# Each 1024-column dot of the expert layer as two instructions of 512 columns

## The reference

```python
experts = e1 * PEER_KEYS + e2                  # 16 of 16384 for each of 8 heads: 128 rows per token
g = jax.nn.softmax(vs, axis=-1)
act = jax.nn.gelu(jnp.einsum('nd,nhkd->nhk', xb, peer_u[experts]), approximate=False)
return jnp.einsum('nhk,nhkd->nd', g * act, peer_v[experts])
```

## Time and profile before

| what | value |
|---|---|
| median of 3 runs | 3529.66 us (3528.91 to 3529.8) |
| profiled execution: its own time | 3546.85 us |
| profiled execution: its span | 3545.1 us |
| busy: PE, DVE, POOL, ACT | 2524.3, 2375.2, 2386.3, 433.4 us |
| DMA | 1321.73 MB, mean 373 GB/s |
| of it gathers | 1107.43 MB |
| mean granted clock of the tensor engine | 0.797 of full speed |

### The profile page before, as it was taken

One profiled execution on the slowest core, in us unless ns is written; L12 is line 12 of the kernel. 1 busy time (PEld: TensorE's weight loads), 2 busy tenths in 40 slices (PEclk: granted clock), 3 DMA queues, 4 the chain that ended last, 5 costly groups with the idle time before them and its releaser, 6 DMA issues.

```text
span 3545.1 us, 35490 instructions
## 1 busy us (share of the span) xinstructions
PE 2524.3 (71%) x11828; PEld 1278.0 (36%) x11828; DVE 2375.2 (67%) x6243; ACT 433.4 (12%) x980; POOL 2386.3 (67%) x2118
## 2 busy tenths in 40 slices
PE   6758566788756786696766677697766777667566
PEld 5634123553432344362332234463332234324100
DVE  4586667767668786867578765767478666847641
ACT  1101100113101221111001110111001110000000
POOL 0155775567757777657767776657767776678876
PEclk8778778898877789897777888898887788766657
DMA  6478999999999999999999999999999999999999
GB/s 251 167 274 317 375 341 408 373 365 377 385 406 341 369 348 410 397 385 388 396 411 408 392 382 407 406 374 400 394 411 396 399 380 407 401 410 403 328 378 353
DMA packets 373369, 1321.73 MB, mean 373 GB/s; under 512 B 60962, under 2 KB 72418, under 8 KB 352962
## 3 DMA queue, kind: packets, MB, share of 16 engines
q0 software_dynamic: 304128, 1107.43, 80.9%
q1 hardware_dynamic: 69058, 212.03, 15.4%
HBM read 1311.41 MB, written 7.88 MB: 372 GB/s over the span
## 4 chain that ended last, share of the span: by engine, by line
POOL 28%; PE 23%; DMA 21%; DVE 14%; issue 11%; SPq 1%; ACT 1%; DVEq 0%; POOLq 0%; ACTq 0%
POOL v_ring L823 14%; POOL u_ring L810 13%; DMA v_ring<-down_rows,codesT 12%; DMA u_ring<-up_rows,codes 6%; PE ps L868 6%; PE ps L931 5%; DMA wbuf<-weights 4%; DVE u_ring L1780 3%; DVE arena L1750 3%; PE ps L921 2%; PE ps L1131 2%; PE ps L1184 2%; DVE idx L1750 1%; DVE top_c L1750 1%; DVE top_v L1750 1%
## 5 line engine op out<-in xcount | busy, mean ns | idle before, releaser
L1780 DVE CUSTOM_DVE_ANT_0 u_ring<-u_ring,xn 128x1024 f32<-128x1024 f32 x1056 | 1263.7, 1220 | 671.1 <-DMA u_ring<-up_rows,codes 670.4
L810 POOL DMA_INDIRECT u_ring<-up_rows,codes x1056 | 1197.0, 1134 | 663.0 <-issue 304.3
L868 PE MATMUL ps<-v_ring,Z 128*32 128x512 f32 x4096 | 1097.8, 755 | 671.9 <-DMA v_ring<-down_rows,codesT 535.0
L823 POOL DMA_INDIRECT v_ring<-down_rows,codesT x1056 | 1188.1, 1125 | 480.2 <-issue 271.7
L868 PEld LDWEIGHTS ps<-v_ring,Z 128*32 128x32 f32 x4096 | 147.3, 120 | 1294.0 <-DMA v_ring<-down_rows,codesT 997.9
L1131 PEld LDWEIGHTS ps<-xT,wbuf 128*128 128x128 f32 x2176 | 309.1, 227 | 185.7 <-issue 118.0
L1131 PE MATMUL ps<-xT,wbuf 128*128 128x128 f32 (+1 forms) x2176 | 334.3, 316 | 47.8 <-DMA wbuf<-weights 47.8
L931 PE MATMUL ps<-wbuf,xT 128*128 128x256 f32 (+2 forms) x1184 | 294.6, 408 | 69.4 <-DMA wbuf<-weights 41.2
L931 PEld LDWEIGHTS ps<-wbuf,xT 128*128 128x128 f32 (+1 forms) x1184 | 231.0, 202 | 150.4 <-DMA wbuf<-weights 45.9
L1750 DVE MAX8 vals<-arena 128x8 f32<-128x128 f32 (+1 forms) x288 | 69.0, 281 | 82.9 <-ACT arena L1564 82.3
L1087 PE MATMUL ps<-kT,qT 96*128 96x512 f32 (+3 forms) x192 | 104.8, 666 | 24.4 <-DVE nb L1754 20.9
(11 more groups left out here) (336 smaller groups left out, 2444.7 us busy)
## 6 DMA issues: line engine op xcount, KB each, us to landing
wbuf<-weights SPq DMA_DIRECT2D x142, 1024.0 KB, 8.2
u_ring<-up_rows,codes POOLq DMA_INDIRECT x1056, 9.0
v_ring<-down_rows,codesT POOLq DMA_INDIRECT x1056, 8.9
u_ring<-weights SPq DMA_DIRECT2D x8, 1024.0 KB, 13.8
v_ring<-weights SPq DMA_DIRECT2D x8, 1024.0 KB, 14.2
wbuf<-weights SPq DMA_DIRECT2D x9, 768.0 KB, 8.2
resid<-x_prompt SPq DMA_DIRECT2D x8, 512.0 KB, 6.8
table<-decay_in SPq DMA_DIRECT2D x8, 512.0 KB, 10.1
```

The costliest lines, as they stand in the source:

```text
L810: pool.indirect_dma_start(out=u_ring[:, i % U_RING, :], out_offset=None, in_=up_rows, in_offset=bass.IndirectOffsetOnAxis(ap=codes[:, t % ...
L823: pool.indirect_dma_start(out=v_ring[:, v % V_RING, :], out_offset=None, in_=down_rows, in_offset=bass.IndirectOffsetOnAxis(ap=codesT[:, t ...
L868: mm = pe.matmul(acc[q:q + 32, half, :], (Zs if t == TILES else Z)[:, at:at + GS], v_ring[:, v % V_RING, half * 512:(half + 1) * 512], sta ...
L1780: dve.tensor_tensor_reduce(u, u, xn[:, t % 2], 1.0, 0.0, ALU.mult, ALU.add, dots[:, k:k + 1]).then_inc(dot_done, 1)
```

## The change

The dot of one slot is done as two instructions, over columns 0 to 511 and 512 to 1023. The first half's sum goes to a new tile `dots_2` (32 columns, one group), the second half's to `dots`, and only the second raises `dot_done`. After the last slot of a group the vector engine waits for that slot's own `dot_done`, adds `dots_2` to `dots` for the 32 columns and raises a new semaphore `dots_summed`, for which the gelu now waits. Ahead of the first slot of a group it waits for its last noted step, so that `dots_2` isn't overwritten while it is still read. A group is GS = 32 slots here (the change's short description speaks of sixteen). The tile `coefs` is gone: the product with the gates is written over `gelus`, and transposed from there.

```diff
--- before.py
+++ after.py
@@ -290,8 +290,8 @@
         codes = sb("codes", [P, 2, SLOTS], U32)
         gates = sb("gates", [P, 2, SLOTS])
         dots = sb("dots", [P, SLOTS])
+        dots_2 = sb("dots_2", [P, GS])
         gelus = sb("gelus", [P, SLOTS])
-        coefs = sb("coefs", [P, SLOTS])
 
         dec_in = table[:, :].rearrange("p (h i) -> p h i", h=H)
         def piece_of(t, w):
@@ -465,6 +465,7 @@
         u_in = [sem(f"u_in_{i}") for i in range(U_RING)]
         v_in = [sem(f"v_in_{i}") for i in range(V_RING)]
         dot_done = sem("dot_done")
+        dots_summed = sem("dots_summed")
         gelu_done = sem("gelu_done")
         coefT_done = sem("coefT_done")
         Z_ready = sem("Z_ready")
@@ -1344,7 +1345,7 @@
 
             def gelu(t, g):
 
-                act.wait_ge(dot_done, t * SLOTS + (g + 1) * GS)
+                act.wait_ge(dots_summed, group_no(t, g) + 1)
                 at = slice(g * GS, (g + 1) * GS)
                 act.activation(gelus[:, at], dots[:, at], ACT.Gelu).then_inc(gelu_done, 1)
 
@@ -1769,16 +1770,24 @@
                 dve.wait_ge(gelu_done, group_no(t, g) + 1)
                 if group_no(t, g) >= 2:
                     dve.wait_ge(Z_ready, group_no(t, g) - 1)
-                do(dve.tensor_tensor, coefs[:, at], gelus[:, at], gates[:, t % 2, at], ALU.mult)
-                do_signal(coefT_done, group_no(t, g) + 1, dve.transpose, coefT[:, g % 2], coefs[:, at])
+                do(dve.tensor_tensor, gelus[:, at], gelus[:, at], gates[:, t % 2, at], ALU.mult)
+                do_signal(coefT_done, group_no(t, g) + 1, dve.transpose, coefT[:, g % 2], gelus[:, at])
 
             def dot(t, k):
 
                 i = t * SLOTS + k
                 dve.wait_ge(u_in[i % U_RING], 16 * (i // U_RING + 1))
-                u = u_ring[:, i % U_RING, :]
-                dve.tensor_tensor_reduce(u, u, xn[:, t % 2], 1.0, 0.0, ALU.mult, ALU.add,
-                                         dots[:, k:k + 1]).then_inc(dot_done, 1)
+                if k % GS == 0:
+                    own.wait()
+                for half, into in ((0, dots_2[:, k % GS:k % GS + 1]), (1, dots[:, k:k + 1])):
+                    of = slice(half * 512, half * 512 + 512)
+                    u = u_ring[:, i % U_RING, of]
+                    ins = dve.tensor_tensor_reduce(u, u, xn[:, t % 2, of], 1.0, 0.0, ALU.mult, ALU.add, into)
+                ins.then_inc(dot_done, 1)
+                if k % GS == GS - 1:
+                    at = slice(k + 1 - GS, k + 1)
+                    dve.wait_ge(dot_done, i + 1)
+                    do_signal(dots_summed, i // GS + 1, dve.tensor_tensor, dots[:, at], dots[:, at], dots_2[:], ALU.add)
 
             def expert_slots(done, upto):
 
```

## The result

The changed kernel takes 3480.01 us in the median of 4 runs (3475.02 to 3489.79), the kernel before 3529.73 in 4 runs beside them: a ratio of 0.9859, with a 95% interval of 0.9835 to 0.9883, so 49.7 us less. The forecast was 42 us less. The profiled execution took 3479.65 us with a span of 3477.9. It lies at the median, where that of the kernel before lay 17 us above its own; spans compared with each other therefore show 67 us, and 17 of these say nothing of the change.

A forecast was written before the change was run, and what follows sets the result against it. The prediction took DMA at 411 GB/s as the main bound, with GpSimd's gather pace in eight stretches. Dots and sums +15 and gathers -57 gave -42 us: 3505 profiled, 3488 without a profile, range 3445 to 3550.

The forecast's parts named there:

- The bound: DMA at 411 GB/s sets most of the time; in eight stretches GpSimd's pace issuing gathers is the bound or very near.
- the eight stretches: Parts of the timeline, 1700 us in all, where GpSimd's busy time plus 0.30 us per gather fills the stretch.
- excess: Gathers' time over 0.938 us each: 404 us in the whole kernel, 252 us of it in the eight stretches.
- The dots' cost: Two instructions add 0.079 us per dot, 83 us; with the sums 94 us, of which +15 on the path.
- The sums: Adding dots_2 to dots for each group of 32: about 0.35 us, 33 times, 11 us; 3 us on the path.
- What the gathers gain: Shorter waits of gathers inside dots: 30% of 404 us, about 120; 76 in the eight stretches, three quarters kept, -57 us.
- The mechanism: A gather begun in a dot waits for its end; caught in the first half, it is freed 0.61 us sooner.
- The lock over the seam: Rival: gathers stay held across both halves, 1.30 us instead of 1.22; +41 us, about 3570; chance 0.15.
- The hidden gain: Rival: DMA bounds the eight stretches after all, only the dots' cost is left, 3537 to 3545 us; chance 0.11.
- The vector engine as the bound: Rival: all 94 us of added vector work on the path with no gain, 3624 us; chance 0.02.
- A sign that misled: Sign of being wrong: GpSimd idle time put down to dots above 166 us means the 94 us are on the path.

The follow-up runs named there:

- no_sum: The changed kernel without the waits and the addition for each group, so the gelu takes the second half's sums alone; 3479.1 us, ratio 0.9868.
- pad_2: The kernel before, coefs dropped, its dot still one instruction, with two one-column vector instructions that nobody reads behind each dot; 3471.3 us, ratio 0.9822.
- pad: The kernel before, coefs dropped, its dot still one instruction, with one one-column vector instruction that nobody reads behind each dot; 3474.2 us, ratio 0.9839.
- one_input: The kernel before with its dot replaced by a plain sum of the U row, without the product with xn (one SBUF input); 3437.0 us, ratio 0.9741.
- seam_896: The changed kernel with the split moved: 896 columns first, then 128; 3464.5 us, ratio 0.9828.
- quarters: Against the kernel before: each dot as four instructions of 256 columns with four accumulators, and two additions for each group; 3513.5 us, ratio 0.9961.

## Why the forecast held, point by point

**The bound.** Right for four of the eight stretches: there GpSimd's pace was what kept the rate under 411 GB/s, and with shorter gathers they run within 1 to 3 of it. The next bound was named too, the DMA rate. From 300 to 500 the rate rose as forecast (353 to 375). From 3100 on it did not (379 to 380), though that stretch held 64 of the 252 us of excess and was named as one where it would rise.

**The dots' cost.** Right in busy time: +94 us forecast, 93.4 measured, halves of 0.69 us 0.61 apart. The sums take 192 ns each and no time that can be measured (no_sum). Of the 94 us I put 15 on the path. No run takes that term by itself. Dots are on the chain for 7% of the span after, 243 us or about 200 dots, and at 0.079 that is 16 us, while pad_2 shows 57 us more for nothing that can be told. So I estimate it between nothing and some 20 us. The Trainium skill (VectorE: DVE Perf Modes, "The TRN2 errata") gives (N + 151)/0.96 ns for one instruction, and its fixed 157 ns would have made the dots 166 us dearer, an estimate from that figure; back to back the rows show 83. For single instructions the trace agrees (691 ns by the formula, 686 here).

**What the gathers gain.** Right in sign and mostly in place; its size and its reason were wrong, and these two errors partly cancelled, so that it is in part luck that the total came out 8 us from the measured one. The step "I take 30% of the 404 us, about 120" was mis-sized: 251 us went away, 62%, and the means fell to 1020 and 1001 ns, not to 1075. I had thought of starts as spread by chance over one dot, with squares. But they are tied to the dots before: the end that frees one gather sets the start of the next. Had I put 62% in, 156 of the 252 us in the stretches, each part capped by its own room (122 in all) and taken at three quarters, it would have been about -92, and the forecast some 3453, below the medians of all kernels here that still multiply. What is missing there is that excess and time aren't in proportion: pad takes 122 us of excess away and gains 56 us, the halves take 251 and gain 50 to 57, one_input takes 381 and gains 92.

**The mechanism.** "A gather caught in the first half now waits for that half's end, 0.61 us sooner" is what happens, and the trace shows it. But pad has no such end and gains as much, and seam_896, where it is worth little, no less. What the runs have in common is that the gathers of 2 us, one for two dots, are gone or few.

**The rivals.** The lock over the seam: in the trace of the kernel before 168 gathers were caught (took over 0.96 us) in a dot that another followed without a gap, and 18 of them were held on past its end; after, with another dot or half following, it was 15 of 304. It exists and is rare; the point at which it decides was half. But it isn't cheap: the gathers over 2.1 us make up 40 of the 153 us of excess that are left, 31 of them at the end of the kernel. The Trainium skill (SBUF — State Buffer, "Who interferes with whom") has the lock held for an instruction; the trace agrees that its end is mostly enough, with these 15 against it. The hidden gain: it did not come, since the rate rose to 408 and more. The vector engine as the bound: no, though quarters shows the way to it. (The chances don't quite follow from each other: by their own words "within" would be 0.065 and slower 0.225, not 0.08 and 0.21.)

**A sign that misled.** I had written that more of GpSimd's idle time put down to dots than 166 us would say that the 94 us are on the path. It is 278 now. But in one_input, whose vector engine does 22 us *less* than before, it is 344.5, and in pad_2, with 124 us more, 207. GpSimd that is quicker comes sooner to the wait that was always behind it. The sign can't tell the two apart.

**What stays open.** Why the place of the seam makes so little difference before the end of the kernel, why the halves have more long-held gathers there than the other seams, and why the rest of the excess (153 us after, 23 in one_input) is still worth some 40 us when the 129 us between pad and after are worth nothing measurable. The tensor engine's mean granted clock was never held fixed: it was 0.793 to 0.808 of full speed in the 33 runs of the kernel before that stand beside the experiments, and 0.797 to 0.807 in the 8 of the changed kernel, which doesn't tell the two apart; but it was higher in the faster one_input (0.805 to 0.819) and lower in quarters (0.788 to 0.797), and whether it is a cause or a consequence there, no run shows.

## What to carry to other kernels

When two engines hold each other up, don't count the busy time they share: write down the distance between the starts on each, and look whether one falls into step with the other. Here 0.07 us more between instructions that come every 1.14 us was worth 56 us of 3530 (pad), and so a split, or one column of work to no purpose, can pay. And before a gain is sized, try what the whole of the suspected cost is worth (one_input: 92 us, with a little less work as well); every version could then be read against that.

## What the runs showed of the hardware

A gather can be held from 0.13 us after its start (an estimate: 0.938 - 0.81). In pad at 202.43 that is 0.12 us after the start of the next dot, and it gets through with no wait; that dot lasts 1.25 us instead of 1.22. In the kernel before at 199.58 it is 0.18 after, and it waits for the rest of the dot. So in pad the two settle at 1.24 us, the gather's own pace (0.94 and 0.30): what was one gather for two dots becomes one for one by itself. An instruction of one column behind a dot lasts 0.148 us, but moves the next dot by only 0.07 (197.54 to 198.75 between accumulator reads, 1.21 for 1.144).
